# GpSimd's low parts of the mixer's weights, in two instructions of 512 columns instead of one of 1024

## The chip, the cores and the metric

The kernel runs on one core of one Trainium2 chip. The metric is device time in microseconds (us), the median of several runs. Within a core five engines work side by side, each through its own list of instructions in order: TensorE (PE, matmuls), VectorE (DVE), ScalarE (ACT), GpSimd (POOL) and SyncE (SP), which here issues the DMAs. They wait for each other only by semaphores.

## What is computed

One layer of an encoder on 512 tokens of width 1024, in fp32: a half-step SwiGLU FFN, a mixer of windowed attention and a bidirectional gated recurrence (HGRN2) side by side, and a second half-step FFN, each with an RMSNorm ahead of it and behind it.

```python
x = x + 0.5 * rmsnorm(swiglu(rmsnorm(x, pre1)), post1)
P = rmsnorm(x, pre_m) @ w_in            # 1024 x 3328: q, k, v | hq, f_fwd, f_bwd, hi, hg
att = rmsnorm(windowed_gqa_sink(rope(q), rope(k), v, sink), w)
f = lb + (1 - lb) * sigmoid(f_logit)    # per direction
o = scan(sigmoid(hq), 1 - f, silu(hi), log f)    # forward + backward, chunked
x = x + rmsnorm(concat(att, rmsnorm(o) * silu(hg)) @ w_out, post_m)
x = x + 0.5 * rmsnorm(swiglu(rmsnorm(x, pre2)), post2)
```

## The kernel before

Every weight matrix is cut into units of 128 x 1024 numbers, read through four slots (`raw`, NSLOT = 4). fp32 precision is had from three matmuls on two parts of each operand. For each unit SP loads `raw`; ACT writes the high part, `WH` = `raw` rounded (line 427, `hi`, which adds 1 to `hi_done`); POOL writes the low part, `WL` = `raw` - `WH` (line 387, `lo`, which waits for `hi_done` and adds 1 to `lo_done`); and PE, which waits for `lo_done`, multiplies X-high by WH, X-low by WH and X-high by WL (lines 741 to 743, or 748 to 750 with the operands' roles exchanged). SP waits for `lo_done` too before it loads the slot again.

The program is FFN 1, then the mixer's input projection with the recurrence (26 units, MIX + 0 to MIX + 25), then the attention with the output projection (8 units, OUT + 0 to OUT + 7, of which the last four go to EH and EL), then FFN 2. The order of everything is written out. The parts that the prediction speaks of are these:

- The mixer's opening. Units 0 to 3 hold the values of the recurrence (`hi`). PE runs `wide` on them for the first two blocks of 128 tokens while ACT and DVE still finish the third and fourth block's norms: line 1160 adds the FFN's output to X, line 1172 makes the normed block YB, PE turns it (line 768), ACT and DVE split it into XH (481) and XL (1181). ACT does the high parts of units 0 to 3 between those steps (unit 2's and 3's only behind `split_high` of a block).
- The tree. `mixer_schedule` interleaves, for each of four heads, eleven score steps (`scores`, lines 904, 908, 913, 919) with halves of later units. For a head, `gates` (DVE, lines 1273 to 1275) makes the queries and `KS`, the sum of both directions' keys. `grow` (DVE, 1309, 1315, 1320) multiplies decays into the keys and the queries of the next level. `mix_keys` (ACT, 590) copies the keys that line 1315 has made to `KM`, and PE multiplies them (908). `take_level` (DVE, 1335) puts the product under a mask. Line 1353 begins the rotation of a q or k unit. Weight units stand three ahead: when the tree runs, POOL makes unit n + 3 while PE multiplies unit n.

POOL's list in this part is: 30 units' low parts (MIX + 0 to MIX + 25 and OUT + 0 to OUT + 3), then four products for the gate (line 405, `HGATE`, 512 columns each), then EL.

Of the kernel before, what the change touches and what calls it, by code (L numbers as in the profile page):

```python
# [21 lines left out]
NSLOT = 4  # L22
# [3 lines left out]
SLOT = KD * P  # L26
# [11 lines left out]
MIX = N_UP + N_DOWN  # L38
# [97 lines left out]
def encoder_layer(nc, io, out):  # L136
    fp32, f32r, u8 = mybir.dt.float32, mybir.dt.float32r, mybir.dt.uint8
    ALU, ACT, AX = mybir.AluOpType, mybir.ActivationFunctionType, mybir.AxisListType
    ctx = ExitStack()
    with ctx:  # L140
        def sb(name, shape, dt=fp32, to=ctx):
            return to.enter_context(nc.sbuf_tensor(name, shape, dt))

        def sem(name):
            return ctx.enter_context(nc.semaphore(name))
# [17 lines left out]
        raw = sb("raw", [P, NSLOT, SLOT])  # L163
        WH, WL = sb("WH", [P, NSLOT, SLOT], f32r), sb("WL", [P, NSLOT, SLOT], f32r)
# [14 lines left out]
        def place(*wanted):  # L179
# [10 lines left out]
            ("swap", [P, P], fp32))  # L190

        EH, EL, *_, S, PT, AT = place(
            ("EH", [P, 4, SLOT], f32r), ("EL", [P, 4, SLOT], f32r), *[(n + "_", s, d) for n, s, d in common],
            ("S", [P, 2, HQ, 3 * P], fp32), ("PT", [P, 2, 3 * P], fp32), ("AT", [P, 2, TOK], fp32))
        *_, HGATE = place(("V_", [P, TT, TOK], fp32), ("W_", [P, 2, 4, TOK], fp32), ("HGATE", [P, TT, TOK], fp32))

        MC = slice((TT - 1) * P, TT * P)
# [10 lines left out]
        hi_done, lo_done = sem("hi_done"), sem("lo_done")  # L208
# [171 lines left out]
        @block.gpsimd  # L380
        def _(pool):
            def lo(n, quarter=0):

                pool.wait_ge(hi_done, quarter * NSLOT + (n + 1))
                s = n % NSLOT
                high, low = (EH[:, n - OUT - 4, :], EL[:, n - OUT - 4, :]) if OUT + 4 <= n < FFN2 else (WH[:, s, :], WL[:, s, :])
                pool.tensor_tensor(low, raw[:, s, :], high.bitcast(fp32), ALU.subtract).then_inc(lo_done, 1)  # L387

            def lo_ffn(first):
                for b in range(NSLOT):  # L390
                    lo(first + b)
                with pool.Fori(0, KF // 2 - 1) as i:
                    for b in range(NSLOT):
                        lo(first + NSLOT + b, i)
                for u in range(N_DOWN):
                    lo(first + N_UP + u)

            lo_ffn(FFN1)
            for u in range(MIX_UNITS + 4):
                lo(MIX + u)  # L400

            for c in range(TT):
                heads = HGATE[:, c, :].rearrange("p (h v) -> p h v", h=NH)
                pool.wait_ge(wide_taken, TT + c + 1)
                pool.tensor_tensor(heads, heads, HGN[:, :].unsqueeze(1).broadcast_to([P, NH, P]), ALU.mult).then_inc(pchain, 1)
            pool.wait_ge(hg_final, TT)
            for u in range(4, KD):
                lo(OUT + u)
            lo_ffn(FFN2)
# [327 lines left out]
        def _(pe):  # L737
# [285 lines left out]
            def att_turn(b, n):  # L1023

                _, nk = keys_of(b)
                pe.wait_ge(s_exp, HQ * b + n + 1)
                if 4 * b + n // 2:
                    pe.wait_ge((pt_even, pt_odd)[n % 2], 4 * b + n // 2)
                else:
                    pe.wait_ge(wide_taken, TT + n % 2 + 1)  # L1030
                for c in range(nk):
                    mm = nc.tensor.transpose(ps[n % 2][:, chunk(c)], S[:, b % 2, n, chunk(c)], ident[:, :])  # L1032
                mm.then_inc(pt_ready, 1)
# [496 lines left out]
```

## Time and profile before

| | |
|---|---|
| median of 3 runs | 1173.91 us (1173.68 to 1175.23) |
| span of the profiled execution, from first to last instruction | 1172.6 us |
| PE busy | 1094.4 us (93%) |
| POOL busy | 406.6 us (35%), 174 instructions |
| mixer's opening and tree | about 386 to 650 us of the span |

The median lies 1.3 us above the span of the profiled execution. A time on this kernel's rows is counted from the span's start. Durations of one instruction in a group's row are means in ns; in the rows of the timeline they are us. An instruction of DVE is fetched while the one before it ends, so neighbours on DVE overlap in the rows by some 0.08 us.

### The profile page before, as it was taken

To read this page: it belongs to the slowest core of one execution; us is meant where nothing else is said; L and a number is where in the kernel's file an instruction comes from. 1 tells how busy PE (TensorE), PEld (TensorE's weight loads), DVE (VectorE), ACT (ScalarE), POOL (GpSimd) and SP (SyncE) were. 2 spreads that over 40 slices of the span, in tenths; PEclk is the share of its full clock that TensorE was granted. 3 is DMA by queue.
4 is the path that set the end of the run, shared out by engine and by line. 5 is a ranking of instruction groups with operands and counts; after the bars stand their busy time and mean duration, and the time that the engine had idled before them with its cause. 6 is when DMAs were issued, how large, how long until landed. Compare 5 with 4: busy or idle time off the path is not lost.

```text
span 1172.6 us, 13192 instructions
## 1 busy us (share of the span) xinstructions
PE 1094.4 (93%) x5075; PEld 895.9 (76%) x5075; DVE 457.9 (39%) x627; ACT 349.5 (30%) x547; POOL 406.6 (35%) x174
## 2 busy tenths in 40 slices
PE   6999999999999588898899789988999999999997
PEld 5988888888888467687787356667888888888886
DVE  4434434430003504755675543345444344340003
ACT  6222222222133423333322444434322222221311
POOL 3444444444442333222123130003544444444440
PEclk9999999999999889898899558998999999999999
DMA  6333333333331332111111120002333333333311
GB/s 202 108 89 107 89 93 104 90 105 128 96 102 54 105 90 73 55 39 52 54 54 55 54 72 1 1 1 72 109 107 90 90 107 89 99 99 109 106 54 72
DMA packets 133369, 96.06 MB, mean 82 GB/s; under 512 B 11457, under 2 KB 116433, under 8 KB 133330
## 3 DMA queue, kind: packets, MB, share of 16 engines
q1 hardware_dynamic: 133008, 95.43, 27.1%
q8 instruction: 27, 0.44, 0.2%
q10 hardware_dynamic: 322, 0.08, 0.0%
q14 instruction: 12, 0.10, 0.0%
HBM read 93.41 MB, written 2.10 MB: 81 GB/s over the span
## 4 chain that ended last, share of the span: by engine, by line
PE 87%; DVE 5%; ACT 4%; issue 2%; POOL 1%; DMA 1%; ACTq 0%; DVEq 0%
PE ps L741 16%; PE ps L743 16%; PE ps L742 16%; PE ps L748 9%; PE ps L750 9%; PE ps L749 9%; PE ps L1020 2%; PE ps L908 2%; PE ps L1048 2%; PE ps L1032 1%; PE ps L941 1%; ACT JK L449 1%; DVE KS L1275 1%; POOL WL L387 1%; PE ps L768 1%
## 5 line engine op out<-in xcount | busy, mean ns | idle before, releaser
L387 POOL TENSOR_TENSOR WL<-raw,WH 128x1024 fp32r<-128x1024 f32 x162 | 392.2, 2423 | 712.9 <-ACT WH L427 712.9
L741 PE MATMUL ps<-XH,WH 128*128 128x512 f32 (+1 forms) x912 | 350.2, 384 | 4.2 <-POOL WL L387 4.2
L742 PE MATMUL ps<-XL,WH 128*128 128x512 f32 (+1 forms) x912 | 346.0, 379 | 0.0
L743 PE MATMUL ps<-XH,WL 128*128 128x512 f32 (+1 forms) x912 | 345.8, 379 | 0.0
L427 ACT ACTIVATE WH<-raw 128x1024 fp32r<-128x1024 f32 x162 | 170.7, 1056 | 346.2 <-PE ps L743 184.9
L741 PEld LDWEIGHTS ps<-XH,WH 128*128 128x128 f32 x912 | 175.8, 193 | 34.9 <-issue 4.5
L743 PEld LDWEIGHTS ps<-XH,WL 128*128 128x128 f32 x912 | 174.9, 192 | 31.7
L742 PEld LDWEIGHTS ps<-XL,WH 128*128 128x128 f32 x912 | 175.7, 193 | 30.7
L748 PE MATMUL ps<-WH,hh 128*128 128x512 f32 x352 | 137.0, 389 | 0.0
L750 PE MATMUL ps<-WL,hh 128*128 128x512 f32 x352 | 136.9, 389 | 0.0
L749 PE MATMUL ps<-WH,hl 128*128 128x512 f32 x352 | 136.9, 389 | 0.0
L1200 DVE TENSOR_TENSOR hl<-SQ,hh 128x512 f32 x44 | 118.6, 2696 | 5.4
L1143 DVE TENSOR_TENSOR YB<-ps,TMP 128x512 f32<-128x512 f32 x24 | 16.6, 691 | 213.7 <-ACT JK L449 212.9
L1196 DVE TENSOR_TENSOR SQ<-ps,TMP 128x512 f32<-128x512 f32 x44 | 30.4, 692 | 169.6 <-PE ps L743 169.6
L491 ACT ACTIVATE SQX<-ps 128x512 f32<-128x512 f32 x44 | 26.3, 598 | 193.6 <-PE ps L743 193.6
L748 PEld LDWEIGHTS ps<-WH,hh 128*128 128x128 f32 x352 | 66.1, 188 | 13.8
L749 PEld LDWEIGHTS ps<-WH,hl 128*128 128x128 f32 x352 | 66.1, 188 | 13.7
L750 PEld LDWEIGHTS ps<-WL,hh 128*128 128x128 f32 x352 | 66.1, 188 | 13.6
L1193 DVE TENSOR_TENSOR TMP<-ps,SQX 128x512 f32<-128x512 f32 x44 | 30.4, 691 | 96.1 <-ACT SQX L491 96.1
L748 PE MATMUL ps<-WH,XH 128*128 128x512 f32 x96 | 44.8, 467 | 14.5 <-POOL WL L387 11.9
L908 PE MATMUL ps<-W,KM 128*128 128x128 f32 x224 | 33.1, 294 | 14.3 <-ACT KM L590 14.1
L908 PEld LDWEIGHTS ps<-W,KM 128*128 128x128 f32 x224 | 30.9, 205 | 19.4 <-issue 18.1
(132 smaller groups left out, 924.6 us busy)
## 6 DMA issues: line engine op xcount, KB each, us to landing
raw<-ffn_w_gate SPq DMA_DIRECT2D x44, 512.0 KB, 3.7
raw<-ffn_w_up SPq DMA_DIRECT2D x44, 512.0 KB, 3.7
raw<-ffn_w_down SPq DMA_DIRECT2D x44, 512.0 KB, 3.7
raw<-w_in SPq DMA_DIRECT2D x22, 512.0 KB, 3.7
raw<-w_out SPq DMA_DIRECT2D x8, 512.0 KB, 3.3
X<-x SPq DMA_DIRECT2D x4, 512.0 KB, 6.7
raw<-w_in SPq DMA_DIRECT2D x8, 256.0 KB, 3.3
out<-X SPq DMA_DIRECT2D x8, 256.0 KB, 2.0
```

Source lines behind the costliest of these rows:

```text
L387: pool.tensor_tensor(low, raw[:, s, :], high.bitcast(fp32), ALU.subtract).then_inc(lo_done, 1)
L427: nc.scalar.activation(to, raw[:, s, :], ACT.Copy).then_inc(hi_done, 1)
L741: nc.tensor.matmul(dst, WH[:, s, w], xh, start=first, stop=False)
L742: nc.tensor.matmul(dst, WH[:, s, w], xl, start=False, stop=False)
L743: return nc.tensor.matmul(dst, WL[:, s, w], xh, start=False, stop=last)
L748: nc.tensor.matmul(dst, xh, wh, start=first, stop=False)
L749: nc.tensor.matmul(dst, xl, wh, start=False, stop=False)
L750: return nc.tensor.matmul(dst, xh, wl, start=False, stop=last)
L908: mm = nc.tensor.matmul(sides[:, c], KM[:, (g - 1) % 2, chunk(c)], level_queries(h, g - 1, c), start=True, stop=True)
L1193: nc.vector.tensor_tensor(TMP[:, a, :], ps[2 * a][:, :], SQX[:, a, :], ALU.mult).then_inc(gate_taken, 1)
L1196: nc.vector.tensor_tensor(SQ[:, a, :], ps[2 * a + 1][:, :], TMP[:, a, :], ALU.mult).then_inc(up_scaled, 1)
L1200: nc.vector.tensor_tensor(hl[:, j, :], SQ[:, a, :], hh[:, j, :].bitcast(fp32), ALU.subtract).then_inc(h_ready, 1)
```

## The change

A new function makes the low part of a unit with two `tensor_tensor` instructions, on columns 0 to 511 and 512 to 1023, and only the second adds 1 to `lo_done`. It is used for the 30 units MIX + 0 to MIX + 25 and OUT + 0 to OUT + 3. The FFNs' units and the four EL units keep `lo`.

```diff
             lo_ffn(FFN1)
+            def lo_by_parts(n):
+
+                pool.wait_ge(hi_done, n + 1)
+                s = n % NSLOT
+                for p in range(2):
+                    f = slice(p * (SLOT // 2), (p + 1) * (SLOT // 2))
+                    ins = pool.tensor_tensor(WL[:, s, f], raw[:, s, f], WH[:, s, f].bitcast(fp32), ALU.subtract)
+                ins.then_inc(lo_done, 1)
+
             for u in range(MIX_UNITS + 4):
-                lo(MIX + u)
+                lo_by_parts(MIX + u)
```

POOL's list between FFN 1's loop and the loop of FFN 2, before (-) and now (+); line 405 before is line 414 now:

```order
 L392 REGISTER_ALU
 L392 COMPARE_AND_BRANCH
-L387 TENSOR_TENSOR WL<-raw,WH 128x1024 x52
-L405 TENSOR_TENSOR HGATE<-HGATE,HGN 128x512 x4
+L387 TENSOR_TENSOR WL<-raw,WH 128x1024 x22
+L405 TENSOR_TENSOR WL<-raw,WH 128x512 x60
+L414 TENSOR_TENSOR HGATE<-HGATE,HGN 128x512 x4
 L387 TENSOR_TENSOR EL<-raw,EH 128x1024 x4
 L387 TENSOR_TENSOR WL<-raw,WH 128x1024 x4
```

The 22 units of FFN 1's second half stay as they were; the 30 behind them have become 60 instructions of half the width. Nothing moves past anything else, and no other engine's list changes.

## Rows read from the trace of the kernel before

**Rows 1.** The page: the span, and each engine's busy time

```profile
span 1172.6 us, 13192 instructions
PE 1094.4 (93%) x5075; PEld 895.9 (76%) x5075; DVE 457.9 (39%) x627; ACT 349.5 (30%) x547; POOL 406.6 (35%) x174
```

**Rows 2.** Waits of PE, 380 to 650 us: total, times, longest

```profile
PE ps L908 <- ACT KM L590: 14.1, 7, 4.2
PE ps L748 <- POOL WL L387: 11.9, 3, 5.9
PE ps L741 <- POOL WL L387: 4.2, 1, 4.2
PE ps L904 <- DVE KS L1275: 3.7, 1, 3.7
...
PE ps L919 <- DVE W L1320: 1.0, 1, 1.0
...
PE ps L908 <- issue: 0.2, 1, 0.2
```

**Rows 3.** Timeline of POOL, 440 to 860 us: start, us, what

```profile
647.01 4.94 POOL L405 TENSOR_TENSOR HGATE<-HGATE,HGN 128x512 f32<-128x512 f32 x4 [1.91 <-DVE HGATE L1342]
678.71 9.27 POOL L387 TENSOR_TENSOR EL<-raw,EH 128x1024 fp32r<-128x1024 f32 x4 [26.76 <-ACT EH L427]
```

**Rows 4.** Timelines of DVE and POOL in the opening, 389 to 398 us

```profile
389.13 1.11 DVE L1160 SCALAR_TENSOR_TENSOR X<-YB,stats,X 128x512 f32<-128x512 f32 x1
389.64 2.83 POOL L387 TENSOR_TENSOR WL<-raw,WH 128x1024 fp32r<-128x1024 f32 x1
390.16 2.85 DVE L1160 SCALAR_TENSOR_TENSOR X<-YB,stats,X 128x512 f32<-128x512 f32 x1
...
397.20 0.75 DVE L1172 SCALAR_TENSOR_TENSOR YB<-X,stats,SQ 128x512 f32<-128x512 f32 x1
...
397.29 2.88 POOL L387 TENSOR_TENSOR WL<-raw,WH 128x1024 fp32r<-128x1024 f32 x1 [4.82 <-ACT WH L427]
...
397.87 2.84 DVE L1172 SCALAR_TENSOR_TENSOR YB<-X,stats,SQ 128x512 f32<-128x512 f32 x1
```

**Rows 5.** Timelines of POOL and DVE at head 0's KS

```profile
451.86 2.57 POOL L387 TENSOR_TENSOR WL<-raw,WH 128x1024 fp32r<-128x1024 f32 x1 [3.05 <-ACT WH L427]
452.15 2.83 DVE L1275 TENSOR_TENSOR KS<-W 128x512 f32<-128x512 f32 x1
456.92 0.69 DVE L1327 TENSOR_TENSOR SD<-ps,ident 128x512 f32<-128x512 f32 x1 [1.94 <-PE ps L904]
```

**Rows 6.** Timeline of DVE at head 1's KS

```profile
479.21 2.83 DVE L1275 TENSOR_TENSOR KS<-W 128x512 f32<-128x512 f32 x1
481.96 0.18 DVE L1309 TENSOR_TENSOR GT<-GT 128x32 f32<-128x32 f32 x1
482.06 0.68 DVE L1315 TENSOR_TENSOR W<-W,GT 128x512 f32<-128x512 f32 x1
```

**Rows 7.** Timelines of POOL, DVE and PE, head 3, 608 to 617 us

```profile
608.98 2.69 POOL L387 TENSOR_TENSOR WL<-raw,WH 128x1024 fp32r<-128x1024 f32 x1 [11.45 <-ACT WH L427]
609.33 2.89 DVE L1320 TENSOR_TENSOR W<-W,GT 128x512 f32<-128x512 f32 x1
613.24 0.71 DVE L1353 TENSOR_TENSOR SQ<-TMP,rope 128x512 f32<-128x512 f32 x1
617.02 0.35 PE L908 MATMUL ps<-W,KM 128*128 128x128 f32 x1 [0.82 <-ACT KM L590]
```

**Rows 8.** Timelines of POOL and DVE, head 3, from 633 us

```profile
633.42 2.71 POOL L387 TENSOR_TENSOR WL<-raw,WH 128x1024 fp32r<-128x1024 f32 x1 [4.61 <-ACT WH L427]
633.80 2.87 DVE L1320 TENSOR_TENSOR W<-W,GT 128x512 f32<-128x512 f32 x1
```

**Rows 9.** Windows of PE: busy time, then granted clock, DMA share, GB/s

```profile
400.22:404.40 4.18, 4.18 (x11) 0.59 0.43 125
455.03:458.90 3.87, 3.87 (x14) 0.56 0.49 140
```

## The prediction

> **What bounds the kernel now.** I read the page first: PE is busy for 1094.4 of the 1172.6 us span, POOL for 406.6 [rows 1]. So the change can pay or cost only where PE stands still in the mixer, and the second view is PE's waits there [rows 2]. Three kinds matter. PE waits four times for a low part itself: 11.9 us in three waits and 4.2 us in one, all in the opening, where ACT's high part, POOL's low part and PE's matmul follow each other with nothing between. Everywhere else units are made ahead, and no wait of PE names POOL. PE waits 3.7 us for `KS` (head 0). And it waits 14.1 us for `KM`, in seven waits of up to 4.2 us, and 1.0 us for the last queries (line 1320): products of DVE, directly or by ACT.
>
> The third view, the timelines of DVE and POOL side by side, shows why a POOL instruction that nobody waits for reaches those last waits. `KS` is a sum of 512 columns and takes 2.83 us, where a DVE product of 512 columns takes 0.68 to 0.69 [rows 5, 6]. It starts 0.29 us behind POOL's instruction at 451.86, which ends at 454.43; `KS` ends at 454.98, 0.55 later. The same is seen at 390.16, 397.87, 609.33 and 633.80: each of these DVE instructions, all with two inputs in SBUF, ends 0.54 or 0.55 us behind the POOL instruction that it met [rows 4, 7, 8]. So a DVE instruction of this kind stands still until POOL's whole instruction is over, and then does its 0.55 us. It works the other way too: POOL's own instruction is lengthened (2.83 and 2.88 us against 9.27 / 4 = 2.32 undisturbed [rows 3, 4]) when DVE came first. And they take turns: at 389.13 DVE queued behind one unit, got in at 389.7 between two POOL instructions that followed each other, and the second POOL instruction lost some 0.5 us; at 397.20 POOL in its turn got in between two DVE instructions [rows 4].
>
> The Trainium skill, SBUF — State Buffer, section "SBUF: two separate sides", calls this pair of ports an exclusive lock that the winner holds for its whole instruction. The rows agree, with 0.54 to 0.55 us as the tail. By a rule of shared bandwidth instead, halving an instruction would free nothing.
>
> **What the change does.** It halves the piece for which the ports are held. A DVE instruction that arrives early in a unit waits for one piece only; in return the second piece has to wait for DVE, and the unit is ready later.
>
> *Price of a split.* Not shown for this operation. Nearest rows: four instructions of 512 columns in a row took 4.94 us, 1.235 each; the widths of 1024 took 2.32 each [rows 3]. Two pieces then cost 2.47 against 2.32, 0.15 more, the end of the last of four counted in. Below, 0 (only the columns count). Above, 0.3, twice that difference, since line 405 is another operation. I take c = 0.10 a unit, between 0 and the row's 0.15 and nearer to the row.
>
> The Trainium skill, GPSIMD Engine Reference, section "Performance versus the Vector engine", gives 4497 ns for a two-input instruction of 2048 columns. An estimate from it and this trace's width of 1024 would put the fixed part near 0.3 us, and the sum below about 1.5 us higher.
>
> *Opening, losses.* Units 0, 3 and 4 meet no DVE instruction on PE's path: 3 x 0.10 = 0.30. Unit 2, at 397.29, holds up line 1172's second half, queued at 397.87. With pieces, DVE gets in between them and the second piece waits as the unit at 389.64 did, 2.83 - 2.32 = 0.5 [rows 3, 4]: 0.5 + 0.10 = 0.60, all of it on PE's path, as PE waits for this unit and ACT's later steps wait for PE. Line 1172 and, at 390.16, line 1160 end about 1 us earlier, but what follows them waits for PE's transposes, which wait for the units: nothing gained. Opening: +0.90.
>
> *Head 0's KS, gain.* The first piece ends 1.17 + 0.05 after POOL really starts, instead of 2.34: KS ends 1.12 us earlier. What is next on DVE (line 1327, one input in PSUM) waits for PE [rows 5], so the second piece bothers nobody. PE waits 3.7 us for just this: -1.12.
>
> *The other three KS, no gain.* Same stretch, but behind KS two more instructions with two SBUF inputs stand ready, lines 1309 and 1315, and it is 1315's result that ACT turns into `KM`, PE's three longest waits [rows 2, 6]. KS gets in earlier, the second piece takes its turn, and 1309 stands behind that. POOL's two pieces, KS and 1315 all have to pass before `KM` in either order, so the sum is the same plus the split: 3 x 0.10 = +0.30.
>
> *Head 3, 609 to 621, gain.* Line 1320 at 609.33 is let in after the first piece and ends near 611.0 instead of 612.2. Line 1335 behind it reads PSUM and runs beside the second piece; line 1353 follows at about 612.2 instead of 613.24, and the chain to `KM` moves up by about 1.1. PE waits 0.82 us for it [rows 7]; that goes. At the next step, where the unit behind this one meets line 1320 again, PE waits 0.2, which the views put down to issue [rows 2]; I count it in. -1.02.
>
> *Head 3, 633, gain.* Line 1320 at 633.80 ends about 1.1 us earlier; PE's wait for it is 1.0 [rows 2, 8] and goes. -1.00.
>
> About nine more meetings lie where PE is not waiting: in each the DVE instruction behind the blocked one meets the second piece, and comes out where it was. SP's loads are released 0.1 to 0.6 us later, under three units of lead. FFN 2 is untouched.
>
> Sum: 0.90 + 0.30 - 1.12 - 1.02 - 1.00 = **-1.94 us**. The profiled span becomes 1170.7; the median stands 1.3 above it, so 1172.0. That is 0.16%, under the 0.2% (2.3 us) that a measurement of this kernel can tell. With c = 0 the sum is about -2.8; each 0.1 of c costs seven units' worth and a little of the gains, about 0.85, so c = 0.3 gives about -0.2. The forecast's own range is 1171.1 to 1173.7.
>
> **The rivals.**
>
> *No turn between pieces* (0.12). If the second piece takes the ports at once, DVE waits as before and only the split is paid: about 11 places on the path x 0.10 = +1.1, 1175.0. For it: the second piece needs no semaphore and may be fetched early. Against it: DVE did get in between two whole units at 389.7 [rows 4].
>
> *DVE passes in a row* (0.08). If KS, 1309 and 1315 all go before the second piece, the three long waits fall by about 1.1 each in place of rising by 0.1: 3.6 us more, 1168.4. Against it: POOL got in between two neighbouring DVE instructions at 397.8 [rows 4].
>
> *The clock* (0.10). Behind head 0's KS the granted clock was 0.56 for 3.87 us, the lower level of 1.2 GHz for most of it [rows 9]. With the wait at 2.6 us instead of 3.7 it might not fall: 3.87 x 0.44 = 1.7 us more, 1170.3. Against it: behind unit 2, whose wait is one of the two that together make 11.9 - 5.9 = 6.0 [rows 2], it was 0.59 all the same [rows 9].
>
> *The split costs more* (0.07), the one on the other side. If a piece has a large fixed part, all places on the path pay it, and the pieces of unit 0, 2, 3 and 4 most plainly. The sum crosses zero at c of about 0.33 and reaches +2.3 at about 0.6, that is 1.47 us for a piece: 1176.3. Against it: 1.235 for the row of 512 columns [rows 3].
>
> **How the numbers follow.** My forecast 0.63, the rivals 0.12, 0.08, 0.10 and 0.07. Faster by over 0.2% (below 1171.6): the second and third rival and an eighth of the forecast (c near 0), some 0.28. Slower by over 0.2% (above 1176.3): most of the last, 0.05. Within: 0.67. The range goes from the clock case with the measurement's slack, 1169.9, to the case without turns, 1175.1; outside lie the case of 1168.4 and that above 1176.
>
> **What would show it.** In the changed kernel's trace: pieces of about 1.2 us; head 0's KS near 1.7 us and PE's wait ahead of line 904 near 2.6; the other three KS also near 1.7, but line 1309 or 1315 behind them lengthened to about 1.3, and PE's waits for `KM` still 4.2 to 4.4; unit 2 from first start to last end about 3.5 us; PE's waits at lines 919 and 908 in head 3 gone. I am wrong if `KS` stays at 2.8, if 1315 follows it at once, if a piece takes over 1.4, or if the clock's windows differ.

## The result

The changed kernel takes 1162.3 us (median of 4 runs, 1160.1 to 1163.3) against 1174.6 (1173.7 to 1176.3) for the one before on the same chip: ratio 0.989, 95% interval [0.988, 0.991]. That is 12.3 us less, where 1.9 were forecast, and it lies outside the forecast's range. One of the runs of the kernel before and one of the kernel with one unit in pieces below (1392 and 1251 us) fell into the chip's slower state and are left out of all figures here.

The page of the changed kernel has the same two rows as [rows 1]:

```profile
span 1161.5 us, 13222 instructions
...
PE 1085.2 (93%) x5075; PEld 890.1 (77%) x5075; DVE 449.5 (39%) x627; ACT 349.0 (30%) x547; POOL 417.9 (36%) x204
```

The span is 11.1 us shorter. The page shows the same 5075 matmuls on PE, but it is busy for 1085.2 us instead of 1094.4: 9.2 us less. What PE spends idle went from 1172.6 - 1094.4 = 78.2 to 76.3, 1.9 us less. So PE's idle time changed by just what was forecast, which is closer than this measure can tell: the five kernels profiled with the old waits have 78.2 to 78.9 us of it, and the one below with the opening alone in pieces has 77.8, though its waits are 0.9 us longer. The rest, five sixths of the gain, is matmuls that ran faster: the clock. Windows of PE by stage show where. Each row gives the stretch, its length, PE's busy time, the granted clock, DMA share and GB/s; the stages are the opening (from the end of PE's first wait for a low part to the end of its wait for head 0's KS), the tree, the attention with the output projection, and FFN 2. The kernel before:

```profile
389.74:455.03 65.29, 51.42 (x196) 0.86 0.28 81
455.03:649.34 194.31, 174.39 (x910) 0.94 0.20 57
649.34:802.09 152.75, 134.28 (x577) 0.78 0.09 26
802.09:1166.53 364.44, 360.55 (x1662) 0.99 0.31 92
```

The changed kernel:

```profile
390.79:456.23 65.44, 51.77 (x197) 0.86 0.28 81
456.23:645.27 189.04, 171.27 (x911) 0.95 0.20 58
645.27:791.50 146.23, 127.54 (x577) 0.81 0.09 27
791.50:1155.48 363.98, 359.97 (x1662) 1.00 0.30 93
```

The tree is 5.3 us shorter: 2.2 of it idle, 3.1 busy. The attention is 6.5 us shorter, all of it busy time (6.7), though no piece of the change lies in it: all 30 units are done by then. Its granted clock is 0.81 instead of 0.78. FFN 1, the same code in both, went the other way. PE begins its weights at 19.6 us in both, but is through with them 0.9 us later in the changed kernel. These windows of PE hold the difference, eight matmuls of some 0.12 us; the kernel before, then the changed one:

```profile
20.00:24.00 4.00, 4.00 (x29) 1.00 0.45 131
```

```profile
20.00:24.00 4.00, 4.00 (x21) 1.00 0.46 131
```

Matmuls of one shape start 0.21 us apart until 21.9 us in the kernel before and until 24.0 us in the changed one, and 0.12 us apart behind that. The clock column has no lower value there, but the near halving of the distance is that between the clock's two levels. So I take it that the clock rose at another moment of the same work in two executions, and that the 0.9 us of FFN 1 is such a difference too.

The steps that the forecast named are all in the trace. Waits of PE in the changed kernel, to be laid beside [rows 2] (line 750 here is 741 there, 757 is 748, 913 is 904, 917 is 908):

```profile
PE ps L917 <- ACT KM L599: 13.3, 6, 4.2
PE ps L757 <- POOL WL L405: 12.8, 3, 6.0
PE ps L750 <- POOL WL L405: 4.3, 1, 4.3
...
PE ps L913 <- DVE KS L1284: 2.6, 1, 2.6
```

The wait for KS went from 3.7 to 2.6; the waits for low parts from 16.1 to 17.1 together; the wait of 1.0 for line 1320's result and the 0.2 put down to issue are gone, and one of the seven for KM. The three long waits for KM are as they were: 4.2. Head 1's KS (line 1284, before 1275) and what follows it, in DVE's timeline:

```profile
480.37 1.75 DVE L1284 TENSOR_TENSOR KS<-W 128x512 f32<-128x512 f32 x1
482.04 1.25 DVE L1318 TENSOR_TENSOR GT<-GT 128x32 f32<-128x32 f32 x1
483.21 0.68 DVE L1324 TENSOR_TENSOR W<-W,GT 128x512 f32<-128x512 f32 x1
```

KS is let in after the first piece (1.75 in place of the 2.83 of [rows 6]); then the small product of 32 columns stands behind the second piece (1.25 in place of 0.18), and line 1324 starts where 1315 did, counted from KS's start (2.84 against 2.85 us). And unit 2 of the opening, POOL's and DVE's timelines:

```profile
398.82 1.80 POOL L405 TENSOR_TENSOR WL<-raw,WH 128x512 fp32r<-128x512 f32 x1 [4.70 <-ACT WH L436]
...
399.40 1.76 DVE L1181 SCALAR_TENSOR_TENSOR YB<-X,stats,SQ 128x512 f32<-128x512 f32 x1
...
400.58 1.71 POOL L405 TENSOR_TENSOR WL<-raw,WH 128x512 fp32r<-128x512 f32 x1
```

It ends 3.47 us after its start, 0.59 later than the 2.88 of [rows 4].

So the open question was the clock. These windows of PE show what changed. The kernel before:

```profile
483.55:486.90 3.35, 3.35 (x12) 0.50 0.33 98
486.90:490.30 3.40, 3.40 (x12) 0.61 0.02 5
...
649.90:700.00 50.10, 41.47 (x114) 0.50 0.17 52
...
724.00:736.00 12.00, 11.71 (x38) 0.57 0.01 3
```

The changed kernel, the same places in its own time:

```profile
484.70:488.05 3.35, 3.35 (x12) 0.52 0.49 143
488.05:491.40 3.35, 3.35 (x20) 0.97 0.02 5
645.27:692.90 47.63, 38.77 (x103) 0.50 0.20 59
...
719.00:731.00 12.00, 12.00 (x58) 0.86 0.01 3
```

In both, PE had stood idle for 4.2 us before 483.55 and 484.70 and for 3.6 before the attention. In the kernel before, the clock then stayed at the lower level (1.2 GHz) for some 6 us, in the changed one for 3.5; in the attention it stayed there until 701 against 693, and a second low stretch in the attention was 10 us against 3.

### The profile page after: what moved, and what is told of

Its sections match the earlier page's. It is cut to its first block, busy times and chain, and to the rows that moved or that the text cites. A ratio compares the mean times of both kernels' runs of the same rounds, so it can differ in the third digit from the quotient of the medians.

```text
span 1161.5 us, 13222 instructions
## 1 busy us (share of the span) xinstructions
PE 1085.2 (93%) x5075; PEld 890.1 (77%) x5075; DVE 449.5 (39%) x627; ACT 349.0 (30%) x547; POOL 417.9 (36%) x204
## 4 chain that ended last, share of the span: by engine, by line
PE 88%; ACT 4%; DVE 4%; issue 2%; POOL 1%; DMA 1%; ACTq 0%; DVEq 0%
PE ps L750 16%; PE ps L751 16%; PE ps L752 16%; PE ps L757 10%; PE ps L759 9%; PE ps L758 9%; PE ps L1029 2%; PE ps L917 2%; PE ps L1057 2%; PE ps L950 1%; PE ps L1041 1%; ACT JK L458 1%; POOL WL L405 1%; ACT WH L436 1%; PE ps L777 1%
## 5 line engine op out<-in xcount | busy, mean ns | idle before, releaser
L387 POOL TENSOR_TENSOR WL<-raw,WH 128x1024 fp32r<-128x1024 f32 x132 | 317.7, 2408 | 499.9 <-ACT WH L436 499.9
L405 POOL TENSOR_TENSOR WL<-raw,WH 128x512 fp32r<-128x512 f32 x60 | 85.7, 1452 | 190.6 <-ACT WH L436 190.6
```

The lines of the kernel that those rows point to most:

```text
L405: ins = pool.tensor_tensor(WL[:, s, f], raw[:, s, f], WH[:, s, f].bitcast(fp32), ALU.subtract)
```

## The experiments

There are two theories of the attention's gain. **Arrival**: how long the clock stays low behind an idle stretch depends on the moment at which PE reaches that stretch; the change only moved the moment. **Tree**: what the changed tree did ahead of it (its shorter waits, its faster matmuls) lets the clock rise earlier. Beside them stands the forecast's own question, which units gain and which lose.

### The units apart: the tree alone, the opening alone

```diff
             for u in range(MIX_UNITS + 4):
-                lo_by_parts(MIX + u)
+                (lo_by_parts if u > 4 else lo)(MIX + u)
```

Expected of the tree alone:

> Pieces only for the units from MIX+5 on; the five units of the opening stay whole. Wait theory: the opening's loss goes (PE's four waits for low parts fall from 17.1 to 16.1 us, unit 2's second half no longer late), the tree keeps its gains (KS 1.75 us, head 3's waits at lines 917 and 928 gone): 0.9 to 1.7 us below the changed kernel as far as waits go, 1160.5 to 1161.5. Arrival theory (the low clock in the attention depends on when that stage is reached): the stage is reached another 1 us earlier than in the changed kernel and its low-clock time may be anything between the two kernels' (31 to 38 us of the window from 650 to 800), so 1158 to 1168.

Expected of the opening alone:

> Pieces only for units MIX+0 to MIX+4. Wait theory: the opening loses about 1.0 to 1.7 us (unit 2 ends 0.6 us later, units 0, 3 and 4 by 0.1 to 0.15 each), the tree gains nothing: 1175.0 to 1176.5. If the gain of 12 us came from the opening (pieces let the norms' DVE steps through), it would be near 1162.

Measured: the tree alone 1162.3 us, ratio 0.9885 [0.9869, 0.9902]; the opening alone 1174.1, ratio 0.9992 [0.9983, 1.0002], no difference. (It has `u <= 4` in that line.) The gain is the tree's units' doing. The tree-only kernel, which does without the opening's loss, is not faster than the whole change. The windows of tree and attention in its profiled execution:

```profile
454.20:641.78 187.58, 169.80 (x911) 0.96 0.20 59
641.78:792.00 150.22, 131.52 (x577) 0.79 0.09 26
```

Its tree is 1.5 us shorter than the changed kernel's and its attention 4.0 longer, with the same code in both stages. A tree with all the pieces did not bring 146 us here, which speaks against the tree theory. But this was the slowest of its four runs (1164.3 us at a mean granted clock of 0.953; the others 1161.4 to 1162.5 at 0.957), so the others' attention may well have been shorter. The opening's own loss, which I expected to see as 1175.0 to 1176.5, is there in PE's waits for low parts (17.0 us for 16.1) but not in the total.

### More work behind the changed tree, less behind the old one

Head 3's `values` (line 941) are the last matmuls ahead of the attention, some 0.9 us and eight of the profile's matmuls for each block of 128 tokens. The kernel of the first expectation repeats all four blocks, on the changed kernel (32 more matmuls, not the 16 that the expectation names); the second does the last block alone, on the kernel before, and leaves out the other three.

```diff
-                for t in range(TT):
+                for t in (*range(TT), *range(TT if h == NH - 1 else 0)):
```

```diff
-                for t in range(TT):
+                for t in range(TT - 1 if h == NH - 1 else 0, TT):
```

> The changed kernel, with the 16 small matmuls of head 3's values done twice, the same result: PE reaches the attention 3.6 us later, the wait of 3.6 us between tree and attention is unchanged. If the attention's low clock depends on the moment at which it is reached: about as long a low stretch as in the kernel before, 1162.3 + 3.6 + 6 = 1172. If it depends on what the tree did ahead of it (its shorter waits): 1165.9, just the added work.

> The kernel before, with head 3's values done for the last block of 128 tokens only (12 of 16 small matmul groups are left out, the recurrence's output for that head is then wrong): PE reaches the attention 2.7 us earlier than in the kernel before, with all waits of the tree as they were. By the moment of arrival: the attention loses its long low stretch, 1174.6 - 2.7 - 6 = 1166. By what the tree did: 1171.9, just the work left out.

Measured: 1165.1 us, 0.9906 [0.9890, 0.9923], and 1164.9 us, 0.9913 [0.9896, 0.9929]. The first came out as the tree theory had it (3.6 us more work, 2.8 us more time), the second as the arrival theory had it (2.7 less work, 10.2 less time, in spite of the old tree). Each theory, in the form I had given it, failed once. The windows for tree and attention, first of the changed kernel with four blocks more, then of the kernel before with three less:

```profile
455.56:648.08 192.52, 174.75 (x943) 0.95 0.21 61
648.08:794.15 146.07, 127.39 (x577) 0.81 0.08 22
```

```profile
454.61:646.23 191.62, 171.60 (x887) 0.94 0.19 54
646.23:792.28 146.05, 127.36 (x576) 0.81 0.10 31
```

The old tree, shortened by 2.7 us of work and no more, is followed by an attention of 146.05 us. So the tree theory falls: the new tree isn't needed for a short attention. The arrival theory stands if "arrival" is not early or late as such but a place in a rhythm: 3.5 us later than the changed kernel is then again a good place. In the kernel before, the granted clock is 1.00 for the first 0.61 us of the attention and falls then; in the changed one it is down at its first matmul.

```profile
649.34:649.95 0.61, 0.61 (x3) 1.00 0.93 302
```

```profile
645.27:645.50 0.23, 0.23 (x1) 0.50 0.96 178
```

I took this as the mark of the place, and forecast four more kernels from it.

### Four kernels at chosen places

Three of the four repeat blocks as above: three blocks on the changed kernel, one on the kernel before, and two on the kernel with the tree alone in pieces (the first line below, with 3, 1 and 2). The fourth has pieces for one unit only (the second edit):

```diff
-                for t in range(TT):
+                for t in (*range(TT), *range(3 if h == NH - 1 else 0)):
```

```diff
-                lo_by_parts(MIX + u)
+                (lo_by_parts if u == 10 else lo)(MIX + u)
```

> The changed kernel with head 3's values done again for three of four blocks, 2.6 to 2.7 us more work on PE ahead of the attention, the same result. Arrival theory, now with a rhythm: the changed kernel, its copy with 3.5 us more and the kernel before with 2.7 us less all spent 146.1 to 146.2 us in the attention, the kernel before and the one with the opening alone in pieces 152.8, the one with the tree alone in pieces 150.2, and this goes with where in a rhythm of the clock's edges the stage begins, not with the tree ahead of it. 2.7 us more puts the changed kernel where the kernel before stood: attention 152.8, total 1162.3 + 2.7 + 6.6 = 1171.6. Tree theory (the changed tree itself makes the attention fast): 1165.0.

Measured 1171.2 us (eight of nine runs between 1170.5 and 1173.7, one 1163.9 with a mean granted clock of 0.957 where the others have 0.947 to 0.950), ratio 0.9964 [0.9945, 0.9982]. The attention:

```profile
646.03:798.82 152.79, 134.28 (x576) 0.78 0.07 21
```

> The kernel before with one block of head 3's values done again, 0.9 us more work, the same result. Arrival theory: the attention begins where the changed kernel's and the shortened one's did, and takes 146.1 in place of 152.8: 1174.8 + 0.9 - 6.6 = 1169.1, faster with more work. Work theory: 1175.7.

Measured 1167.4 us, ratio 0.9937 [0.9920, 0.9954]: 8 us faster than the kernel before, for 0.9 us more work.

```profile
454.54:649.61 195.07, 175.14 (x919) 0.94 0.20 58
649.61:795.62 146.01, 127.31 (x576) 0.81 0.08 25
```

Both came out as the arrival theory has it. 2.7 us more work cost 8.9 us in the changed kernel (on two chips, whose times of the kernel before differ by 0.8), and 0.9 more gained 8 in the one before. The old tree keeps its time plus the block (195.07 against 194.31), and the attention, begun 0.27 us later in the span and with the clock already low, is 6.7 us shorter.

> The kernel before with pieces for one unit only, MIX+10, the one that head 0's KS meets. Waits: PE's wait at line 904 falls from 3.7 to 2.6. By waits alone: 1174.8 - 1.1 = 1173.7. With the clock: the tree begins 1.1 us earlier, as in the changed kernel, so its second and third low stretch shrink from 6.8 to 3.4 us as there (3.4 us of time), and the attention begins in between, as in the kernel with the tree alone in pieces (150.2 for 152.8): 1174.8 - 1.1 - 3.4 - 2.6 = 1167.7.

Measured 1163.8 us, ratio 0.9904 [0.9883, 0.9925]. One unit of the thirty gives over 11 of the 12 us. Of its waits, only the one for KS is shorter, 2.6 us instead of 3.7. Tree and attention:

```profile
453.41:645.58 192.17, 172.26 (x911) 0.96 0.20 57
645.58:792.00 146.42, 127.94 (x576) 0.81 0.09 27
```

The tree is 2.1 us shorter with the clock alone, as its waits (other than KS's, which lies ahead of the window) are the old ones. The attention came out at 146.4 where I had expected 150.2: the clock falls some 0.4 us into it, and this is already on the good side. The first row is this kernel's, the second that of the changed kernel with three blocks more:

```profile
645.96:646.20 0.24, 0.24 (x3) 0.50 0.72 290
```

```profile
646.03:646.54 0.51, 0.51 (x3) 1.00 0.00 0
```

The clock is down from 0.38 us after the attention's first matmul (at 645.58) in the one (146.4 us), and still up until 0.51 us after it (at 646.03) in the other (152.8), where it falls then. The step from 146 to 153 us lies between.

> The kernel with the tree alone in pieces, with two blocks of head 3's values done again, 1.8 us more work, the same result. Arrival theory: the attention begins where it takes 146.1 in place of 150.2: 1162.3 + 1.8 - 4.1 = 1160.0. Work theory: 1164.1.

Measured 1165.0 us, ratio 0.9916 [0.9898, 0.9933]: a miss by 5 us, on the side of the work theory. The profiled execution does have an attention of 146.7 (against 150.2), but its tree is 1.5 us longer than the sum of the tree alone and the two blocks. That execution is also the fastest of the four (1163.4; the others 1164.2 to 1166.1 at a slightly lower mean clock), so it doesn't tell what the attention took at the median.

### The tree's own clock, by work instead of pieces

```diff
                 bank_free(n)
+                if n == 6:
+                    pe.wait_ge(lo_done, MIX + n + 1)
+                    for k in (0, 1, 2):
+                        three(ps[bank_of(n)][:, :], (MIX + n) % NSLOT, k, XH[:, k, :], XL[:, k, :], not k, k == 2)
+                    nc.tensor.matmul(ps[bank_of(n)][:, :], WH[:, (MIX + n) % NSLOT, 0:P], XH[:, 0, :], start=True, stop=True)
                 whole(MIX + n, 0, ps[bank_of(n)])
```

> The kernel before with 10 matmuls of the last unit ahead of the tree done twice, 2.3 us more work on PE, the same result. The tree begins 2.3 us later, which in the rhythm of the clock's edges is where the changed kernel's tree begins. Arrival theory: the tree's low stretches near 483 and 535 us shrink from 6.8 to 3.4 us each, the tree takes about 3.4 less (191 for 194.3) without a single piece, and the attention takes less than 152.8: total between 1167 and 1171. Work theory: 1174.9 + 2.3 = 1177.2.

Measured 1169.2 us, ratio 0.9953 [0.9937, 0.9970]. The ten matmuls more are 2.3 us of work by estimate; there is no piece, and the time is 6.4 us less.

```profile
456.53:648.71 192.18, 172.29 (x911) 0.96 0.20 57
648.71:795.07 146.36, 127.98 (x577) 0.81 0.09 27
```

The tree takes 192.2 instead of 194.3, the same as with the one unit in pieces. I had expected 191. A likely reason, not tested, is that the low stretches begin while PE still waits, so that less of what is saved had been work. The profiled execution is the fastest of the four here too (1166.9; the others 1168.5 to 1170.0 at a mean clock of 0.956 against 0.959). So the gain in the total is sure, and the 146.4 us is that of one execution.

### How common the old kernel's place is

> The kernel before with two blocks of head 3's values done again, 1.8 us more work, the same result. Arrival theory: attention between 146 and 150 us, total 1174.9 + 1.8 - (2.6 to 6.7) = 1170 to 1174; it tells how often a start of the attention is as unlucky as the kernel before's. Work theory: 1176.7.

Measured 1171.0 us, ratio 0.9966 [0.9954, 0.9979], attention 147.3. Of the kernel before with 0, 1, 2 blocks more and with three less, three of four have an attention of 146 to 147.3 us; of all fourteen kernels profiled, three have 152.8 (the one before, the one with the opening alone in pieces, and the one sent there), one 150.2, ten 145.9 to 147.3. The kernel before stood at a bad place, and each of the shifts tried on it behind the opening helped. Laid out by the moment at which the clock falls, counted from the attention's first matmul (read in windows as above; minus is before it), the fourteen profiled executions are these, in us:

| kernels | clock falls | clock back up | second low stretch | attention |
|---|---|---|---|---|
| tree alone with two blocks more | +1.5 | 45.9 | 3 | 146.7 |
| before; opening alone; changed with three blocks more | +0.61, +0.52, +0.51 | 51.7 to 51.8 | 10 | 152.8 |
| one unit; work ahead of the tree | +0.38, +0.26 | 48.2, 48.0 | 3 | 146.4 |
| changed; changed with four more; before with one more; before with three less; four units | -0.03 to -0.47 | 47.3 to 47.8 | 3 | 145.9 to 146.2 |
| quarters; before with two more | -1.45, -1.25 | 46.3, 46.5 | 3 | 147.3 |
| tree alone | -1.8 | 46.0 | 10 | 150.2 |

This is a reading after the fact, of one execution of each kernel. The long stretch follows the order of the places. The second stretch doesn't quite: the first and the last row have the clock back up at the same time, and one has 3 us where the other has 10.

### Quarters, and the four units that matter

```diff
-                for p in range(2):
-                    f = slice(p * (SLOT // 2), (p + 1) * (SLOT // 2))
+                for p in range(4):
+                    f = slice(p * (SLOT // 4), (p + 1) * (SLOT // 4))
```

> The changed kernel with four instructions of 256 columns in place of two of 512. From 2.34 for 1024 and 1.235 for 512, a piece of 256 would take about 0.68 and a unit 2.7. PE's waits: line 904 near 2.1 (2.6 with halves), the three long ones for KM near 3.9 (4.2), the four in the opening together 1.1 to 1.5 us longer; PE idle in all within 1 us of the changed kernel's 76.3. If pieces as such had made the 12 us, twice as many would bring more (below 1158); if the clock did, the total is anywhere between 1160 and 1171.

Measured 1158.3 us, ratio 0.9859 [0.9837, 0.9882], the fastest of all, some 4 us below the changed kernel. Its largest waits, and the tree:

```profile
PE ps L757 <- POOL WL L405: 14.0, 3, 6.8
PE ps L917 <- DVE W L1329: 10.7, 3, 3.6
```

```profile
456.12:639.88 183.76, 167.95 (x911) 0.97 0.20 60
```

PE idle is 1157.6 - 1082.1 = 75.5 us, 0.8 less than with halves: the three long waits are 3.6 instead of 4.2, the opening's are 18.6 together, 1.5 more. DVE's rows show why the long waits fell. Head 1's KS and what follows it:

```profile
480.28 1.21 DVE L1284 TENSOR_TENSOR KS<-W 128x512 f32<-128x512 f32 x1
481.41 0.70 DVE L1318 TENSOR_TENSOR GT<-GT 128x32 f32<-128x32 f32 x1
482.04 0.68 DVE L1324 TENSOR_TENSOR W<-W,GT 128x512 f32<-128x512 f32 x1
```

KS and the small product are each held up by one piece. With halves that was the whole unit, and line 1324 started 2.84 us behind KS; with quarters two pieces are still to come, and it starts 1.76 behind. Here too most of the step from halves is busy time: 1082.1 against 1085.2. Of the tree's 5.3 us, 2.0 are idle time and 3.3 are busy time. Behind the second of the three long waits the clock was low for 3.4 us with halves and isn't with quarters (the changed kernel, then quarters):

```profile
536.00:539.40 3.40, 3.40 (x14) 0.50 0.39 140
```

```profile
534.00:542.00 8.00, 7.75 (x41) 1.00 0.22 68
```

Whether the shorter wait did this or its place isn't shown. The wait of 3.6 us ahead of the attention is as short, and the clock is low behind it in all kernels.

> The kernel before with pieces for four units only, MIX+10, MIX+25, OUT+0 and OUT+2, those that meet DVE instructions for which PE waits. Wait theory: PE idle falls from 78.1 by all the gains and none of the losses, KS 1.1, lines 917 and 928 in head 3 2.0: 75.0. Total by waits alone 1171.8. With the clock, as with the one unit MIX+10 (1164.2): 1162.2 if the attention stays at 146, up to 1169 if it falls on its long one.

```diff
-                lo_by_parts(MIX + u)
+                (lo_by_parts if u in (10, 25, 26, 28) else lo)(MIX + u)
```

Measured 1161.7 us, ratio 0.9892 [0.9875, 0.9910]. PE idle: 1159.2 - 1084.2 = 75.0 us, as forecast from the sum's gains without its losses. It has the changed kernel's time within the runs' spread, with 4 units of 30 in pieces. The opening's units are whole in it.

## Why the prediction was wrong

**The locks and turns: right.** A DVE instruction with two inputs in SBUF is let in between two pieces and the second piece takes its turn before the next: KS is 1.75 us in all four heads, and the next DVE instruction of the kind stands behind the second piece. Both rivals on the order of turns fall.

**The price of a split: nearly right.** 0.10 us a unit was used. PE's three undisturbed waits in the opening grew by 0.14 to 0.15 (5.90 to 6.05, 4.10 to 4.24, 4.15 to 4.30), the 2 x 1.235 - 2.32 of the row, and so by 0.05 more than taken. The estimate near 0.3 from the Trainium skill's figure (GPSIMD Engine Reference, section "Performance versus the Vector engine", 4497 ns for 2048 columns) comes out only with the 2.40 us that a single undisturbed unit lasts in the trace. With the 2.32 of [rows 3], which the forecast used everywhere else, the same estimate is 2 x 2.32 - 4.50 = 0.14, and the measured 0.15 agrees with it.

**Opening +0.90: right.** PE's four waits grew by 1.0 us (16.1 to 17.1), unit 2 by 0.59.

**KS -1.12, the other three KS +0.30, head 3 -1.02 and -1.00: right in kind.** The wait for KS changed by -1.1, and head 3's by all of -0.8, -0.2 and -1.0. The 0.30 did not show: the three long waits were 4.24, 4.24 and 4.22 us and are 4.22, 4.23 and 4.21. The four units that carry these gains, in pieces by themselves, bring idle down by 3.2 us (3.14 in the sum), and the whole change by 1.9 (1.94 in the sum). The agreement to 0.1 is luck, since idle time of kernels with equal waits differs by up to 0.7, but the single waits are sure.

**The step that failed** is the one from waits to time: "Sum: ... = -1.94 us. The profiled span becomes 1170.7". It took PE's matmuls to last as before, apart from the one stretch of the clock rival. They took 9.2 us less. "FFN 2 is untouched" was nearly so (0.5 us), but the attention, which the working doesn't mention, lost 6.7 us of busy time and the tree 3.1 (FFN 1 gave back 0.9 of it and the opening 0.35).

**The clock rival named the right thing at the wrong place.** It asked whether the wait of 2.6 us ahead of head 0's tree would be too short for the clock to fall. It fell all the same (the row below, beside the 0.56 of [rows 9]); what changed were the stretches behind the unchanged waits of 4.2 and 3.6 us, because PE reached them at another moment. Shown by: the old tree with one block more or three less (attention 146 us), the changed tree with three blocks more (152.8 us), and the old tree begun behind ten more matmuls (2.1 us shorter). Its price, "1.7 us", was a single stretch; there are about a dozen, and the one at the attention lasts 50 us. "or if the clock's windows differ" stood among the forecast's signs of being wrong, and it is the one that came.

```profile
456.23:460.10 3.87, 3.87 (x16) 0.66 0.37 107
```

**The range** held no case for this. Its lower end was the clock case of one stretch. Rows of the kernel before that would have told: a granted clock of 0.78 over the 152.8 us of the attention means that 44% of them were at half speed, and nothing in the sum looked at what that could move. One chance was also added up wrong: the parts of "faster by over 0.2%" are 0.08, 0.10 and an eighth of 0.63, which is 0.26 and not 0.28.

What stays open: why the place sets the length of the long stretch (51 against 48 us), beyond that it does; what sets the one of 10 us behind it; and how much of the quarters' further 4 us is their place.

## What to carry to other kernels

An engine that nobody waits for can stall one that somebody waits for, through shared ports; find it by DVE instructions of one shape that take several times their usual time and end a fixed time behind a GpSimd instruction. Each DVE instruction of the kind lets one piece pass. So halves free DVE early only if its next instruction of the kind isn't ready, while quarters helped even where it was. Each cut costs some 0.15 us where PE waits for the unit.

When a kernel's PE has stretches at half clock behind idle stretches, split every measured difference into idle time and busy time of PE first. If the matmuls are the same and busy time moved, the edit has changed moments, not work: then a control that shifts the same stage by a microsecond of harmless work tells how much of the gain belongs to the edit. Here the waits were 1.9 of the 11.1 us of the span, and the old tree with 0.9 us of work more had two thirds of the whole gain without the edit.

## What was unexpected of the hardware

Adding 0.9 us of matmuls ahead of an idle stretch made the kernel 8 us faster. The attention took 152.8 us where the clock fell 0.51 us after its first matmul and 146.4 where it fell 0.38 after it: a tenth of a microsecond in arrival, 6.4 us in time. The same code of FFN 1 ended 0.9 us apart in two executions, in which the matmuls came closer together at 21.9 and at 24.0 us. One run in nine of the kernel with three blocks more took 1163.9 us against 1171.2, at a higher mean clock; it probably fell on the other side of such a step, but it has no trace.

A GpSimd instruction and DVE instructions with two inputs in SBUF take turns at the ports instruction by instruction: KS took 2.83 us against whole units, 1.75 against halves and 1.21 against quarters, where undisturbed DVE products of its shape take 0.68.
